# A macaron block on one core: x loaded by token tiles with its row sums on ScalarE, scale weights queued behind x, and buffers of its own for the normalization of k

## What is computed

```python
def _rms(x, g):
    y = xf * lax.rsqrt(jnp.mean(xf * xf, axis=-1, keepdims=True) + EPS)
    return (y * g.astype(jnp.float32)).astype(x.dtype)
def _modulate(x, g, shift, scale):
    return _rms(x, g) * (1 + scale[:, None, :]) + shift[:, None, :]
...
    mod = cs @ w_ada[l] + b_ada[l]
    sh1, sc1, gt1, shm, scm, gtm, sh2, sc2, gt2 = jnp.split(mod, N_MOD, axis=-1)
    h = _modulate(x, g_norm1[l], sh1, sc1)
    x = x + FFN_RES * gt1[:, None, :] * _swiglu(h, ffn1_w_in[l], ffn1_w_out[l])
    h = _modulate(x, g_norm_mix[l], shm, scm)
    x = x + gtm[:, None, :] * _hybrid_mixer(h, ...)
    h = _modulate(x, g_norm2[l], sh2, sc2)
    x = x + FFN_RES * gt2[:, None, :] * _swiglu(h, ffn2_w_in[l], ffn2_w_out[l])
```

## Time and profile before

| | us |
|---|---|
| median of 3 runs | 2344.71 (2341.88 to 2349.51) |
| the profiled execution | 2341.26 |
| its span | 2339.5 |
| TensorE busy | 2208.4 (94%) |
| VectorE busy | 1085.8 (46%) |
| ScalarE busy | 649.6 (28%) |
| POOL busy | 85.1 (4%) |

### The profile page before, as it was taken

One profiled execution on the slowest core, in us unless ns is written; L12 is line 12 of the kernel. 1 busy time (PEld: TensorE's weight loads), 2 busy tenths in 40 slices (PEclk: granted clock), 3 DMA queues, 4 the chain that ended last, 5 costly groups with the idle time before them and its releaser, 6 DMA issues.

```text
span 2339.5 us, 25894 instructions
## 1 busy us (share of the span) xinstructions
PE 2208.4 (94%) x10577; PEld 1846.1 (79%) x10577; DVE 1085.8 (46%) x1188; ACT 649.6 (28%) x791; POOL 85.1 (4%) x163
## 2 busy tenths in 40 slices
PE   3899999999999989999998998898999999999998
PEld 3778888888888767787887877786888888888887
DVE  4744445433333665655556566835233333323324
ACT  3211111111111245545445445513111111111102
POOL 3010000000000000000000000000000000000000
PEclk6899999999999989999989999998999999999999
DMA  8253232321111111101010101221211111011102
GB/s 310 71 169 99 91 126 91 98 72 54 55 54 45 45 54 33 29 19 28 20 27 19 29 18 28 85 60 50 68 54 48 43 54 45 28 52 54 54 27 72
DMA packets 160643, 145.02 MB, mean 62 GB/s; under 512 B 4532, under 2 KB 144940, under 8 KB 159916
## 3 DMA queue, kind: packets, MB, share of 16 engines
q1 hardware_dynamic: 135028, 78.18, 11.5%
q0 software_dynamic: 17024, 61.09, 7.5%
q10 hardware_dynamic: 8504, 4.47, 0.7%
HBM read 135.07 MB, written 8.65 MB: 61 GB/s over the span
## 4 chain that ended last, share of the span: by engine, by line
PE 83%; DVE 7%; ACT 4%; issue 3%; DMA 2%; ACTq 0%; SPq 0%; DVEq 0%
PE ps L545 25%; PE ps L547 25%; PE ps L546 25%; PE ps L758 2%; DMA x_rows<-in_x_dram 1%; PE ps L560 1%; PE ps L706 1%; DVE neg_max L1477 1%; PE ps L553 1%; PE ps L567 1%; DMA ada_ring<-in_w_ada_dram 1%; ACT probs L1057 1%; PE ps L692 1%; PE ps L695 0%; ACT pT_hi L1065 0%
## 5 line engine op out<-in xcount | busy, mean ns | idle before, releaser
L545 PE MATMUL ps<-h_hi,w_hi 128*128 128x512 f32 x2000 | 795.1, 398 | 16.2 <-DVE h_lo L1344 12.3
L547 PE MATMUL ps<-h_hi,w_lo 128*128 128x512 f32 x2000 | 788.1, 394 | 0.0
L546 PE MATMUL ps<-h_lo,w_hi 128*128 128x512 f32 x2000 | 787.5, 394 | 0.0
L545 PEld LDWEIGHTS ps<-h_hi,w_hi 128*128 128x128 f32 x2000 | 381.4, 191 | 94.3 <-issue 16.6
L547 PEld LDWEIGHTS ps<-h_hi,w_lo 128*128 128x128 f32 x2000 | 380.6, 190 | 81.6
L546 PEld LDWEIGHTS ps<-h_lo,w_hi 128*128 128x128 f32 x2000 | 381.2, 191 | 76.6
L1420 DVE SCALAR_TENSOR_TENSOR xT<-ps,gate,xT 128x1024 f32<-128x1024 f32 x176 | 223.6, 1282 | 181.5 <-PE ps L547 181.5
L545 PE MATMUL ps<-act_hi,w_hi 128*128 128x512 f32 x704 | 274.3, 390 | 0.0
L547 PE MATMUL ps<-act_hi,w_lo 128*128 128x512 f32 x704 | 273.9, 389 | 0.0
L546 PE MATMUL ps<-act_lo,w_hi 128*128 128x512 f32 x704 | 273.9, 389 | 0.0
L1411 DVE TENSOR_TENSOR gated<-ps,gated 128x1024 f32<-128x1024 f32 x44 | 53.9, 1224 | 445.6 <-ACT gated L983 445.6
(11 more groups left out here) (214 smaller groups left out, 1979.4 us busy)
## 6 DMA issues: line engine op xcount, KB each, us to landing
raw<-in_ffn_w_in_dram SPq DMA_DIRECT2D x88, 512.0 KB, 4.7
ada_ring<-in_w_ada_dram POOLq DMA_DIRECT2D x48, 512.0 KB, 5.2
raw<-in_ffn_w_out_dram POOLq DMA_DIRECT2D x42, 512.0 KB, 4.5
raw<-in_w_in_mix_dram SPq DMA_DIRECT2D x29, 512.0 KB, 3.9
ada_first<-in_w_ada_dram POOLq DMA_DIRECT2D x8, 1024.0 KB, 8.6
x_rows<-in_x_dram SPq DMA_DIRECT2D x4, 1024.0 KB, 24.1
ada_second<-in_w_ada_dram POOLq DMA_DIRECT2D x4, 1024.0 KB, 17.0
x_spill<-xT SPq DMA_DIRECT2D x1, 4096.0 KB, 11.1
```

The costliest lines, as they stand in the source:

```text
L545: pe.matmul(dst, whi, mhi, start=start, stop=False)
L546: pe.matmul(dst, whi, mlo, start=False, stop=False)
L547: return pe.matmul(dst, wlo, mhi, start=False, stop=stop)
```

## The change

In the run-up, x is loaded without waiting for the small loads and in four quarters of two token tiles each, all features of a token in one piece. POOL's SH1 loads wait for x's first quarter, its SC1 loads for x's third. SyncE loads the first weights when the third of SC1's four loads is there. TensorE transposes by token tile; ScalarE squares `x_rows` directly, with the sum over features accumulated into `rms`, so that `add_square` and TensorE's column sums are gone from the first norm, and takes root and spread (`first_root`) right behind the last tile, ahead of splitting the weights. VectorE does all of SH1's additions first, the inverse behind SC1's first, reads SH1's vector after four of SC1's, and splits the weights behind SC1's last. In the mixer's rounds that project a next pair, k is squared into `k_stage`, copied into `k_f` and its root kept in `rms_k`; k's squares follow q's spread, ahead of level 5's exponentials; k's sums stand behind q's `turn_back`, ahead of level 5; k's `turn_back` ahead of the last third of `unit_v`; and VectorE takes level 6's difference before `qk_apply` of q, and q's low parts behind the inverse of k. The first pair keeps the shared buffers.

```diff
         mixed = place("mixed", [P, KD, S], at=x_at)[0]
+        k_stage, k_f = [place(n, [P, S], at=x_at + d * 4 * S)[0] for n, d in (("k_stage", 3), ("k_f", 6))]
         KA = HD + 4
...
         chunk_decay = ov("chunk_decay", [P, TT], F32, 83)
+        rms_k = ov("rms_k", [P, 2 * TT], F32, 83.125)
         fg_t, fg_l, fg_F, fg_one = [ov(n, [NH, S], F32, 68 + 4 * j) for j, n in enumerate(("fg_t", "fg_l", "fg_F", "fg_one"))]
...
         qk_rms = InverseRms("qk_rms", HD, 2, 3)
+        k_rms = InverseRms("k_rms", HD, 2, 0, rms_k, qk_rms)
         attn_rms = InverseRms("attn_out_rms", DA, 1, 3)
...
+        def qk_tiles(a, n):
+            return (stage, qk_f) if n == 0 or isinstance(a, int) else (k_stage, k_f)
+        def qk_turn(a, n):
+            return k_rms if n and not isinstance(a, int) else qk_rms, 2 * a + n + 1
         def down_pair(f, g, d):
...
                              g.rearrange("a (r j) -> (a r) j", j=P)).then_inc(s_rows, 16)
-            sp.wait_ge(s_rows, 16 * SMALL_LOADS)
+            x_tiles = x[0].rearrange("(t p) d -> p t d", p=P)
             for q in range(4):
-                cq = slice(q * D // 4, (q + 1) * D // 4)
-                sp.dma_start(x_rows[:, :, cq], x[0].rearrange("(t p) d -> p t d", p=P)[:, :, cq]).then_inc(s_x[q], 16)
+                sp.dma_start(x_rows[:, 2 * q:2 * q + 2, :], x_tiles[:, 2 * q:2 * q + 2, :]).then_inc(s_x[q], 16)
...
+            sp.wait_ge(s_adaL1[KD // 2 - 2], 16)
             load_ffn_chunk(ffn1, 0)
...
                     if v == SH1 and k == 2:
-                        pool.wait_ge(s_rows, 16 * SMALL_LOADS)
+                        pool.wait_ge(s_x[0], 16)
                     if v == SC1 and k == 0:
-                        pool.wait_ge(s_x[0], 16)
+                        pool.wait_ge(s_x[2], 16)
                     pool.dma_start(tiles_[:, k:k + 2, :], ada[:, k:k + 2, v, :]).then_inc(loaded[k // 2], 16)
...
                     turn_back(qk_rms, stage, 2 * i + 3)
+                    qk_sum_next(i, 1)
                 level(i, 5)
...
                 unit_v(8, 14)
+                level(i, 6)
                 if not last_round:
-                    qk_sum_next(i, 1)
-                level(i, 6)
-                unit_v(14, 16)
-                if not last_round:
-                    turn_back(qk_rms, stage, 2 * i + 4)
+                    turn_back(k_rms, k_stage, 2 * i + 4)
                 else:
                     turn_back(attn_rms, orstd, 1)
+                unit_v(14, 16)
                 pe.wait_ge(g_state, 7 * (i + 1))
...
                 if n:
-                    pe.wait_ge(a_n, 2 * i + 3)
-                token_sums(qk_rms, stage)
+                    pe.wait_ge(a_g, 2 * i + 4)
+                token_sums(*(k_rms, k_stage) if n else (qk_rms, stage))
...
             pe.transpose(ps[:, 0, 0, 0:N_ROWS], rows[0:N_ROWS, :], ident[0:N_ROWS, 0:N_ROWS]).then_inc(s_colsT, 1)
-            for d in range(KD):
-                p_ = 1 + d % 3
-                pe.wait_ge(s_x[d // 2], 16)
-                if d >= 3:
-                    pe.wait_ge(s_xT, d - 2)
-                for t in range(TT):
-                    last = pe.transpose(ps[:, p_].rearrange("p h f -> p (h f)")[:, t * P:(t + 1) * P],
-                                        x_rows[:, t, d * P:(d + 1) * P], ident[:, :])
+            for t in range(TT):
+                pe.wait_ge(s_x[t // 2], 16)
+                if t >= 3:
+                    pe.wait_ge(s_xT, t - 2)
+                for d in range(KD):
+                    last = pe.transpose(pair(1 + t % 3)[:, d * P:(d + 1) * P], x_rows[:, t, d * P:(d + 1) * P], ident[:, :])
                 last.then_inc(s_xt, 1)
             pe.wait_ge(s_cols, 1)
-            pe.wait_ge(s_xT, KD - 1)
-            norm_sum(norms[0])
+            pe.wait_ge(s_xT, TT)
             mod_vector(SH1, 1)
...
+            def token_square(t):
+                act.wait_ge(s_x[t // 2], 16)
+                if t >= 2:
+                    act.wait_ge(norms[0].sq, t - 1)
+                act.activation(sq[:, t % 2], x_rows[:, t, :], ACT.Square, accum_out=rms[:, TT + t:TT + t + 1]
+                               ).then_inc(norms[0].sq, 1)
+            def first_root():
+                act.wait_ge(norms[0].sq, TT)
+                act.activation(rms[:, 0:TT], rms[:, TT:2 * TT], ACT.Sqrt, bias=eps_col[:, 0:1], scale=1.0 / D
+                               ).then_inc(x_rms.root, 1)
+                rms_spread(x_rms, rstd, 1)
             def norm_hi(nm, shift):
...
             def qk_squares(a, n, unit, p_, stage_free):
+                squared, with_gain = qk_tiles(a, n)
                 act.wait_ge(m_half, 2 * unit + 2)
...
                     act.wait_ge(g_ot, 1)
-                act.activation(stage[:, :], pair(p_), ACT.Square).then_inc(a_sq, 1)
-                act.activation(qk_f[:, :], pair(p_), ACT.Identity, scale=q_gain[:, n:n + 1]).then_inc(a_g, 1)
+                act.activation(squared[:, :], pair(p_), ACT.Square).then_inc(a_sq, 1)
+                act.activation(with_gain[:, :], pair(p_), ACT.Identity, scale=q_gain[:, n:n + 1]).then_inc(a_g, 1)
...
+                r, turn = qk_turn(a, n)
...
                 act.wait_ge(a_n, 2 * a + n + 1)
-                act.activation((q_st, k_st)[n][e][r, :], stage[r, :], ACT.Copy).then_inc(a_hi, 1)
+                act.activation((q_st, k_st)[n][e][r, :], qk_tiles(a, n)[0][r, :], ACT.Copy).then_inc(a_hi, 1)
...
                     qk_spread(i + 1, 0)
+                    qk_squares(i + 1, 1, n0 + 5, 0, None)
                 level_exp(i, 5)
+                level_exp(i, 6)
                 if not last_round:
...
                     qk_hi(i + 1, 0, 1)
-                level_exp(i, 6)
-                if not last_round:
-                    qk_squares(i + 1, 1, n0 + 5, 0, (a_lo, 2 * i + 3))
                     qk_root(i + 1, 1)
...
             act.activation(lb_e[:, :, :], lb_e[:, :, :], ACT.Exp).then_inc(s_lbe, 1)
-            for d in range(KD):
-                act.wait_ge(s_xt, d + 1)
-                square(norms[0], d, None, 0, pair(1 + d % 3))
-                act.activation(xT[:, d], pair(1 + d % 3), ACT.Copy).then_inc(s_xT, 1)
+            for t in range(TT):
+                token_square(t)
+                act.wait_ge(s_xt, t + 1)
+                act.activation(xT[:, :, t * P:(t + 1) * P], pair(1 + t % 3).rearrange("p (d j) -> p d j", j=P), ACT.Copy
+                               ).then_inc(s_xT, 1)
+            first_root()
             chunk_hi(ffn1, 0, 0)
...
-                dve.wait_ge(qk_rms.turned, 2 * a + n + 1)
-                dve.tensor_tensor(stage[:, :], qk_f[:, :], pair(qk_rms.p_), ALU.mult).then_inc(a_n, 1)
+                (normed, with_gain), (r, turn) = qk_tiles(a, n), qk_turn(a, n)
+                dve.wait_ge(r.turned, turn)
+                dve.tensor_tensor(normed[:, :], with_gain[:, :], pair(r.p_), ALU.mult).then_inc(a_n, 1)
             def qk_lo(a, n):
+                normed = qk_tiles(a, n)[0]
                 for e in range(2):
...
                     dve.wait_ge(a_hi, 4 * a + 2 * n + e + 1)
-                    dve.tensor_tensor(lo_rows, stage[own, :], hi_rows, ALU.subtract)
+                    dve.tensor_tensor(lo_rows, normed[own, :], hi_rows, ALU.subtract)
                     copied = dve.tensor_copy(hi_again, hi_rows)
...
                 level_mul(i, 5)
+                level_sub(i, 6)
                 if not last_round:
...
                 level_copy(i, 4)
-                level_sub(i, 6)
+                level_mul(i, 6)
+                rms_inverse(*(attn_rms, 1) if last_round else (k_rms, 2 * i + 4))
                 if not last_round:
                     qk_lo(i + 1, 0)
-                level_mul(i, 6)
-                rms_inverse(*(attn_rms, 1) if last_round else (qk_rms, 2 * i + 4))
                 level_copy(i, 5)
...
             for k in range(KD):
-                add_square(norms[0], k)
                 ada_first_add(SH1, k)
...
                 ada_first_add(SC1, k)
-                if k == 2:
-                    chunk_lo(ffn1, 0, 0)
-                if k == 4:
+                if k == 0:
                     rms_inverse(x_rms, 1)
-            mod_read(SH1, 1)
+                if k == 3:
+                    mod_read(SH1, 1)
+            chunk_lo(ffn1, 0, 0)
             mod_read(SC1, 1)
```

More of the change, by code:

```diff
@@ L228, in build, with __init__ @@
         class InverseRms:
-            def __init__(self, name, count, blocks, p_):
+            def __init__(self, name, count, blocks, p_, tile=None, signals=None):
                 self.count, self.blocks, self.p_ = count, blocks, p_
-                self.summed = sem(name + "_squares_summed")
-                self.root = sem(name + "_root")
-                self.inverse = sem(name + "_inverse")
-                self.spread = sem(name + "_spread")
-                self.turned = sem(name + "_turned")
+                self.tile = rms if tile is None else tile
+                if signals is None:
```

(10 more changed lines are left out.)

22 lines of the change are left out of this document (11 added, 11 removed).

## The result

| | before | after |
|---|---|---|
| median of 4 runs | 2345.75 us | 2304.82 us (2303.41 to 2307.19) |
| ratio (95% interval) | | 0.9823 (0.9808 to 0.9838) |
| profiled execution, span | 2341.26, 2339.5 us | 2303.41, 2301.7 us |
| mean granted clock | 0.966 | 0.978 |

What follows compares the result with a forecast made beforehand. TensorE, busy 94% of the span, was taken as the bound, so only its waits or low-clock stretches could be won. Gains of 25.5 (run-up), 11 (rounds) and 0.5 (last round) sum to 37: 2344.7 to 2308 us, range 2299 to 2321.

Steps and rivals of the forecast that it cites:

- Run-up, 25.5 forecast: Before the first feed-forward: earlier x and fewer additions start it at 48.1 us, not 73.64, a gain of 25.5 us.
- the two paths that gave the 40: Run-up: VectorE's additions end at 39.7 both by the root plus seven additions and by the loads; taken as 40 us.
- last quarter at about 24: Run-up: x's last quarter lands at about 24 us, its second quarter having the queues alone for 2 us.
- by the loads it is 37 plus two additions: Run-up: SC1's loads end at about 37 us and two VectorE additions follow, ending at 39.7.
- The tail of 8.07 us: Run-up: from the end of VectorE's additions to the first feed-forward matmul the old 8.07 us remain.
- the rival in which half of the run-up's gain is given back there (0.08): Behind the first group: ring buffers of modulation vectors set the pace, half of 25.5 us goes, time 2321; chance 0.08.
- the rival of the gate tiles (0.2): Run-up: first weights share turns with the gate tiles, feed-forward starts at 60.5, gain 13, time 2320 us; chance 0.2.
- Rounds, 11 forecast: Mixer's first three rounds: k's waits go and the clock falls one to two times, a gain of 11 us.
- The wait of 2.0 us goes in each of three rounds: 6.0: Mixer rounds: TensorE no longer waits for k's squares, gaining 6.0 us in all.
- One to two falls: Mixer rounds, around k's sums: the clock drops in one to two of three rounds, each costing 3.4 us.
- the wait moves: Mixer rounds: level 5 or the output products wait instead, rounds bring 0 to 2 us, time 2318; chance 0.12.
- The last round, 0.5 forecast,: Mixer's last round: level 6's difference is computed a copy earlier, gaining 0 to 0.6 us, taken as 0.5.

Runs made afterwards that it cites:

- runup_only: The run-up half of the change alone, with the rounds of the kernel before: median 2321.49 us, ratio 0.9895 to the kernel before.
- experiments 2 and 3: Kernel before with only x's rows lengthened to 4 KB: 2346.14 us in one run; changed kernel with x back in 1 KB rows: 2310.9 us in one run.
- Experiment 5: Changed kernel with the four gate-tile (GT1) loads issued ahead of POOL's constants instead of behind them: 2311.44 us in one run.
- k_only: The half with k's own buffers alone, with the run-up of the kernel before: median 2330.94 us, ratio 0.9930 to the kernel before.
- x_wait: Changed kernel with SyncE's old wait for the small loads put back ahead of x: 2308.16 us in one run.
- k_sums_x3: Changed kernel with k's sums computed three times in each of three rounds, only the last used: 2324.48 us in one run.
- k_old_place: Changed kernel, k's own buffers kept, but k's sums back behind level 5 and VectorE in its old order: median 2318.08 us, ratio 0.9891 to the kernel before.
- k_old_place_2: Changed kernel with k's sums in their old place, but VectorE making level 6's product before q's low parts, these before k's inverse: 2299.1 us in one run.
- weights_first: Changed kernel without SyncE's wait ahead of the first weights, which then stand right behind x: 2309.17 us in one run.

## Why the prediction was right, step by step

**Run-up, 25.5 forecast; 26.3 at the first matmul, 24.5 where the rounds begin, 25.8 by runup_only.** The mechanism was right: the packets' size sets x's share (experiments 2 and 3), and VectorE's additions set the end. That the end fell on the microsecond (39.3, forecast 40) is in part luck, for neither of the two paths that gave the 40 ended last. One path was the root at 30.2 with seven additions behind it. The root was out at 28.55 and VectorE did not wait for it. x had come earlier than worked out ("last quarter at about 24" was 20.6), because it was alone for longer than 2 us: 1.07 MB moved from 10.45 to 13 us, nothing of it for SH1. The other path was "by the loads it is 37 plus two additions". SC1's bytes ended near 35, and VectorE never waited for them. What set the end was a third path, which the prediction did not have: VectorE waits 6.4 us for SH1's second load, until 20.46, and has 14 additions behind it. That load came so late because it is issued behind x's first quarter.

The rest of the run-up came as forecast. The tail of 8.07 us was 8.06. The weights, forecast for 40.5, were there at 39.8, and VectorE was done with them 0.8 us before it could read SC1 (42.99), the cover that was forecast. (The 2048 packets take 4.2 us by the rate of the earlier trace rows, not the 4.1 of the prediction; the 2 us ahead of the first byte, for which it shows no row, were 1.6, from 33.22 to 34.80.) The gate tiles came at 45.35, forecast 45. Of the 26.3 us, 1.8 are gone before the rounds; 1.0 of it is a longer wait for modulation vectors (4.1 for 3.1), the rest was not followed up. So the rival in which half of the run-up's gain is given back there (0.08) fails, though 1.8 us of it happened.

From 24 to 34 us, with one queue at work, the loads moved at 411 GB/s. The Trainium skill, SBUF — State Buffer, section "A bandwidth-pool intuition that's wrong", gives about 358 GB/s from HBM to a core. By that figure the gain was estimated at 22.3; the measurement decides. The 26.3 us at the first matmul exclude 22.3, the interval of runup_only (21 to 29 us) does not.

Casts of 128x64 on POOL took 1.32 us beside VectorE's additions and 0.24 after them, and that delay is what made the rival of the gate tiles (0.2) fail. The Trainium skill, SBUF — State Buffer, section "SBUF: two separate sides", says that a VectorE operation with two inputs in SBUF keeps out a GpSimd operation that reads SBUF for its whole length. The trace agrees, by the two times just given. Experiment 5 shows that the rival would have cost 8.9 us; 12.4 was priced (60.5 less 48.1), because the weights landed at 49.7 there, where 54 was worked out.

**Rounds, 11 forecast; 14.5 by the trace, 16.3 by k_only, 14.2 by the means of the traces.** The size was near, the split was wrong. "The wait of 2.0 us goes in each of three rounds: 6.0" holds for that wait, but TensorE's idle time did not fall by 6: it was 35.7 and 36.4 in the two traces, and fell by 1.9 in the mean. The prediction left out that a TensorE at full clock comes earlier to engines whose clock does not change, as at the transposes of `dec` (up to 1.13 us a round). The level copies cost up to 0.95 us a round, where 0.5 was the bound. The root of k hid behind its 18 matmuls, as forecast: k's transposes wait for nothing. "One to two falls" of the clock at k's sums were none in this trace. The clock paid for all of the 14.5: 15.1 us of busy time. The three falls at k's sums, 3.4 us each, are 10.2 of it; most of the rest is at the end of the round, where the prediction did not look (the 8 us from the sums there stood at 0.79, 0.57, 0.79 and now at 1.00, 0.79, 1.00). So the wait that didn't pay and the clock that paid more than forecast made up for each other, and that is luck. How much of it varies from one execution to the next, x_wait shows: with the same rounds the clock fell twice at k's sums, and the three rounds took 466.8 us, not 459.8. The rival "the wait moves" was right about the waits and wrong about the time.

Why the stretch keeps the clock is not shown. A wait is not needed to lose it (k_sums_x3). Taking the wait for the squares away does not save it (k_old_place, where another wait stood in its place, and k_old_place_2, without any). The changed kernel's order of narrow and wide matmuls lost it in 4 of 21 rounds, and the old order without a wait in 3 of 3, at half the cost of before; that is a difference, but over the three rounds it gave the two kernels the same time.

**The last round, 0.5 forecast,** was not measured apart: between the last round's start and the end 1.2 us were given back.

## What to carry to other kernels

Look at the size of the packets before the order of the loads. Here two queues shared turns, not bytes: x with rows of 1 KB beside loads with rows of 4 KB got a fifth. A wait on a semaphore is the means to keep two loads from sharing at all (weights_first: 2.2 us). When a wait on the bounding engine is removed, compare its total idle time, not that one row: here 5.9 us of waits went, the idle time stayed in the profiled trace and fell by 1.9 us in the mean, and the gain came from the clock. Such a gain should be read from several executions, since the clock falls in other places each time. And when loads have been made early, look at the order of the engine behind them: with VectorE's 24 additions still in their place, x 17 us earlier was worth 3.6.

## What the runs showed of the hardware that was not expected

- The near-equal number of packets of two busy queues, read before from one trace, held in every pair of sizes tried: 905 to 808 and 896 to 894 (4 KB beside 512 B), 817 to 828 (4 KB beside 1 KB), 925 to 851 (4 KB on both). The small ones' bytes were a tenth to a fifth.
- TensorE lost the clock in k_sums_x3 in three rounds of three (0.83, 0.80, 0.78) while it was busy without a wait, with transposes and matmuls of 2 and 64 columns.
- POOL's constants took 26.7 us (18.6 to 45.35) instead of 13.3 with VectorE adding beside them, about one POOL operation passing per addition. The prediction had counted on this; its size, twice the time, is what was new.
